# Prompt attention ordered by query halves of both heads, with two projection quarters behind each product with v

## What is computed

```python
def _fox_attention(q, k, v, c_q, c_k, past):
    ...
        s = jnp.einsum('bqhd,bkhd->bhqk', q_blk, k).astype(jnp.float32) * scale
        s = s + cq_blk.astype(jnp.float32).transpose(0, 2, 1)[..., None] - ckT
        s = jnp.where(k_pos[None, :] <= q_pos[:, None], s, NEG_INF)
        p = jax.nn.softmax(s, axis=-1)
        return jnp.einsum('bhqk,bkhd->bqhd', p.astype(v.dtype), v)
```

## Time and profile before

| | |
|---|---|
| median of 3 executions | 2783.07 us (2780.73 to 2791.97) |
| profiled execution, device time | 2785.51 us |
| its span | 2784.0 us |
| TensorE busy | 2279.1 us, 82% of the span |
| VectorE, ScalarE, GpSimd busy | 1317.5, 1122.8, 214.3 us |
| attention of the 8 pairs | from 185.5 to 1166.2 us of the span |
| mean granted clock of TensorE | 0.906 of full |

### The profile page before, as it was taken

The page is one execution under the profiler, slowest core; times in us unless marked ns, Lnnn a source line. Parts: engine busy times, 40 slices in busy tenths (PEclk is TensorE's granted clock), DMA queues, the critical chain, the costliest instruction groups (busy, mean ns, idle before and its releaser), DMA issues. The chain is left out here.

```text
span 2784.0 us, 36577 instructions
## 1 busy us (share of the span) xinstructions
PE 2279.1 (82%) x11080; PEld 1757.0 (63%) x11080; DVE 1317.5 (47%) x1548; ACT 1122.8 (40%) x1520; POOL 214.3 (8%) x278
## 2 busy tenths in 40 slices
PE   4468787888879797699899959989917999999991
PEld 2447575655657474499888849974515766666660
DVE  4333534444353435421156542111136888777874
ACT  3223333433334333221155642101106777777760
POOL 0210202011010101000012100000020000000002
PEclk9769898989889798799999979999958999999995
DMA  2210202021120201121145632123037999999986
GB/s 83 64 39 1 78 0 78 0 78 39 39 57 21 63 0 55 56 78 45 46 149 174 190 131 77 45 105 135 1 128 260 382 366 366 371 353 369 356 305 233
DMA packets 207115, 377.28 MB, mean 136 GB/s; under 512 B 20508, under 2 KB 128200, under 8 KB 206968
## 3 DMA queue, kind: packets, MB, share of 16 engines
q1 hardware_dynamic: 184680, 302.07, 32.3%
q0 software_dynamic: 18784, 61.92, 7.0%
q10 hardware_dynamic: 3584, 12.58, 1.1%
HBM read 301.87 MB, written 74.66 MB: 135 GB/s over the span
## 5 line engine op out<-in xcount | busy, mean ns | idle before, releaser
L2117 DVE TENSOR_TENSOR e_w_lo<-e_raw,e_w_hi 128x2048 fp32r<-128x2048 f32 x192 | 436.5, 2289 | 126.0 <-ACT e_w_hi L2044 113.8
L2044 ACT CAST e_w_hi<-e_raw 128x2048 fp32r<-128x2048 f32 x192 | 366.6, 1911 | 149.5 <-DMA e_raw<-w_down_e 67.5
L101 PE MATMUL proj_ps<-w_qkv_hi,xh 128*128 128x384 f32 x544 | 219.7, 404 | 33.5 <-PEq L286 19.2
L1133 PE MATMUL out_ps<-mT 128*128 128x512 f32 (+3 forms) x384 | 187.7, 575 | 10.8 <-ACT mT L1333 10.1
L103 PE MATMUL proj_ps<-w_qkv_hi,xl 128*128 128x384 f32 x544 | 186.6, 343 | 0.0
L102 PE MATMUL proj_ps<-w_qkv_lo,xh 128*128 128x384 f32 x544 | 186.1, 342 | 0.0
L1057 PE MATMUL max_ps<-qk_high 66*128 66x512 f32 (+1 forms) x192 | 89.9, 468 | 73.9 <-DVE neg_part L1471 67.4
L101 PEld LDWEIGHTS proj_ps<-w_qkv_hi,xh 128*128 128x128 f32 x544 | 106.4, 196 | 61.3 <-issue 58.3
L1656 PE MATMUL m_prod<-m_w_o,mT 128*128 128x512 f32 (+1 forms) x288 | 128.1, 604 | 12.2 <-DMA m_w_o<-w_o 12.2
L1471 DVE TENSOR_REDUCE neg_part<-max_ps 128x1 f32<-128x512 f32 (+3 forms) x128 | 75.7, 591 | 130.8 <-PE max_ps L1057 69.8
L1333 ACT ACTIVATE mT<-st_ps 128x512 f32<-128x512 f32 x192 | 93.5, 490 | 90.5 <-PE st_ps L1118 51.2
(11 more groups left out here) (402 smaller groups left out, 5364.7 us busy)
## 6 DMA issues: line engine op xcount, KB each, us to landing
e_raw<-w_gate_e SPq DMA_DIRECT2D x64, 1024.0 KB, 14.1
e_raw<-w_up_e SPq DMA_DIRECT2D x64, 1024.0 KB, 14.7
e_raw<-w_down_e SPq DMA_DIRECT2D x64, 1024.0 KB, 13.5
slot_x<-zrows POOLq DMA_DIRECT2D x48, 440.0 KB, 6.4
e_x<-slot_x SPq DMA_DIRECT2D x33, 384.0 KB, 12.1
w_raw<-w_in SPq DMA_DIRECT2D x24, 512.0 KB, 4.5
slot_y<-e_y ACTq DMA_DIRECT2D x32, 384.0 KB, 6.1
slot_y<-zrows POOLq DMA_DIRECT2D x24, 352.0 KB, 9.5
```

The lines of the kernel that those rows point to most:

```text
L101: nc.tensor.matmul(out, a_hi, b_hi, start=start, stop=False)
L1133: te.matmul(out_ps[u % 2][:, q0 - c * BANK:BANK], v_one[:, j, h, :], probsT[s % 2][:, 0:q1 - q0], start=(j == 0), stop=(s == last_step(u)) ...
L2044: sc.copy(w_hi[u][:, :], w.raw[c][:, :]).then_inc(wh_ready, 1)
L2117: v.tensor_tensor(w_lo[u][:, :], w.raw[c][:, :], w_hi[u][:, :], ALU.subtract).then_inc(wl_ready, 1)
```

## The change

Four things change in `attend`, and the work is the same.

- **Units.** They run (head 0, half 0), (head 1, half 0), (head 0, half 1), (head 1, half 1): 4, 4, 8 and 8 steps. The 24 maxima follow that order: 0 to 3 for the first unit, 4 to 7 for the second, 8 to 15 and 16 to 23.
- **Quarters.** All 36 stand right behind `weigh(s)` in steps 0 to 17, two in each. None stands in part 0 any more.
- **Items.** `SLOTS` is new. Before the loop, both heads are turned for the first four tiles only, and 4 maxima are taken instead of 10; in the loop `qk` 2 and 3 are the pair's own (steps 0 and 1 for head 0, 7 and 8 for head 1), `qk` 0 and 1 the next pair's. Eight maxima stand in steps 0 to 3 of the pair, four in steps 18 to 21.
- **GpSimd.** `take_v` copies four tiles at a time and waits for the steps that have used them; its first waits no longer for `kv_ready`, that is for the norms of the next pair.

```diff
-    UNITS = [(0, 0), (0, 1), (1, 0), (1, 1)]
+    UNITS = [(0, 0), (1, 0), (0, 1), (1, 1)]
...
-    PROJECT = {3: (1, 2), 4: (1, 2), 5: (1, 2), 6: (1, 1), 7: (1, 2), 8: (1, 1),
-               9: (1, 2), 10: (1, 1), 11: (1, 2), 12: (1, 2), 13: (1, 1), 14: (1, 2), 15: (1, 2), 16: (0, 1)}
+    PROJECT_STEPS = 18
...
-    SLOTS = {0: ((), (("qk1", 0), ("max", 10))), 1: ((("max", 11),), (("qk1", 1),)),
...
+    SLOTS = {0: ((), (("qk0", 2), ("max", 4))), 1: ((("max", 5),), (("qk0", 3), ("max", 6))),
...
-    FIRST_MAXES = 10
+    FIRST_MAXES = 4
...
-                def take_v(p, h):
-                    po.tensor_copy(v_one[:, :, h, rows_of(h)], v_next[:, 0:PT, rows_of(h)]).then_inc(v_copied[h], 1)
+                def take_v(p, h, half):
+                    tiles = slice(half * HALF, (half + 1) * HALF)
+                    po.tensor_copy(v_one[:, tiles, h, rows_of(h)], v_next[:, tiles, rows_of(h)]).then_inc(v_copied[h], 1)
...
-                    pool.wait_ge(st_ready, i * NS + last_step(1) + 1)
+                    pool.wait_ge(st_ready, i * NS + last_step(2) + 1)
                     alone(pool, g)
                     load_c(i + 1, 0)
+                    taken(HALF)
+                    weighed(last_step(2) - HALF)
+                    take_v(i + 1, 0, 0)
                     copy_high(i + 1, 0, 0)
-                    pool.wait_ge(kv_ready, i * BATCHES + 2 * BATCHES)
-                    alone(pool, g)
-                    pool.wait_ge(pv_done, i * NS + last_step(1) + 1)
-                    alone(pool, g)
-                    take_v(i + 1, 0)
+                    weighed(last_step(3) - HALF)
+                    take_v(i + 1, 1, 0)
                     if more:
                         rest_w(i + 2, 0)
                         rest_w(i + 2, 1)
+                    taken(NT)
+                    take_v(i + 1, 0, 1)
...
-                            if c == 0:
-                                pe.wait_ge(v_copied[h], i + 1)
-                                alone(pe, g)
+                        if j == c * HALF:
+                            pe.wait_ge(v_copied[h], i * 2 + c + 1)
+                            alone(pe, g)
...
-                        counts = PROJECT[s] if ahead and s in PROJECT else (0, 0)
+                        counts = (0, 2) if ahead and s < PROJECT_STEPS else (0, 0)
```

More of the change, by code:

```diff
@@ L808, in attend @@
-    FIRST_MAXES = 10
+    HALF = PT // 2
+    SLOTS = {0: ((), (("qk0", 2), ("max", 4))), 1: ((("max", 5),), (("qk0", 3), ("max", 6))),
+             2: ((("max", 7),), (("rows", 1), ("max", 8))), 3: ((("max", 9),), (("qs", 0), ("max", 10))),
+             4: ((("max", 11),), (("past", 0), ("max", 12))), 5: ((("max", 13),), (("past", 1), ("max", 14))),
+             6: ((("max", 15),), (("rows", 2), ("out", 0))), 7: ((("qk1", 2),), (("ss", 0), ("mean", 0))),
+             8: ((("qk1", 3),), (("sp", 0), ("max", 16))), 9: ((("max", 17), ("root", 0)), (("ss", 1),)),
+             10: ((("max", 18), ("sw", 0)), (("sp", 1),)), 11: ((("max", 19), ("past", 2)), (("sw", 1), ("norm", 0))),
+             12: ((("max", 20),), (("ss", 2), ("max", 21))),
+             13: ((("max", 22), ("sp", 2)), (("past", 3), ("max", 23), ("norm", 1))),
+             14: ((("rows", 3),), (("sw", 2), ("out", 1))), 15: ((), (("out", 2),)),
+             16: ((("qk0", 0),), (("ss", 3),)), 17: ((("qk0", 1),), (("sp", 3), ("mean", 1))),
+             18: ((("max", 0), ("w", 0)), (("sw", 3), ("ss", 4), ("root", 1))),
+             19: ((("max", 1), ("norm", 2)), (("sp", 4), ("w", 1))), 20: ((("max", 2), ("norm", 3)), (("sw", 4),)),
+             21: ((("max", 3),), (("w", 2),)), 22: ((("rows", 0),), (("qk1", 0), ("sum", 0))),
+             23: ((("qk1", 1),), (("o", 0),))}
@@ L809, in attend @@
+    FIRST_MAXES = 4
     NO_TURN = ("max", "out", "mean", "root", "norm", "w", "sum")
-    later = lambda item: item[0] in ("qk0", "mean", "root", "norm", "w") or item == ("rows", 0) or (item[0] == "max" and item[1] < FIRST_MAXES)
+    later = lambda item: item[0] in ("mean", "root", "norm", "w") or item == ("rows", 0) or \
+        (item[0] == "max" and item[1] < FIRST_MAXES) or (item[0] in ("qk0", "qk1") and item[1] < BATCHES // 2)
     items = lambda s, part, ahead: [e for e in SLOTS[s][part] if ahead or not later(e)]
@@ L1081, in _ @@
                     max_chunk(n)
[L1082 to L1084 removed]
+                pe.wait_ge(max_taken, FIRST_MAXES)
+                pe.wait_ge(turn_taken[0], in_bank(BATCHES, 0))
+                turn_rows(0, 0)
                 def step(i, ahead):
@@ L1525, in fill @@
                             h = int(what == "qk1")
-                            p, bank = i + 1 - h, use[item] % 2
+                            p, bank = i + 1 if n < BATCHES // 2 else i, use[item] % 2
                             take_cross(p, h, n, bank)
```

102 lines of the change are left out of this document (49 added, 53 removed), and 3 rows, old and new, of the table SLOTS.

## The result

The changed kernel takes 2837.05 us (median of three runs, 2830.97 to 2858.07) against 2783.07: a ratio of 1.0204, 95% interval 1.0115 to 1.0293. Slower, and 1 us above the range of the prediction. The first fence is the head of the page of its profile. The second is the timeline of TensorE (start, us, instruction, wait ahead of it): first the item `o` of the first and sixth pair, then rows of the third pair.

A forecast was written before the change was run, and what follows sets the result against it. TensorE was taken to wait for rounds through ScalarE and VectorE. Stretches 27.4 + 78.8 + 24.0 = 130.2 against 127.4, +2.8 a pair; 16.8 + 1.1 + 5 - 0.3 = +22.6, giving 2806 us, range 2764 to 2836.

The forecast's parts named there:

- Stretch A: From score(0) to score(4), the start of step 3; forecast to grow from 16.2 to 27.4 us.
- the walk with both falls of the clock: Walk through steps 0 to 2 with the clock falling after both max waits: score(4) at 28.7 us, 25.1 with none.
- the quarters stand ahead of the turn: Steps 0 to 2: quarters are not between turn and max, so hide none of the 2.3 us wait at max 5.
- Stretch B: From score(4) to score(19), the middle of a pair; forecast to fall from 87.2 to 78.8 us.
- the round from max to max is 1.45 us, against 0.8 of work: 0.65 each, five times, 3.3: New waits in the middle of a pair, with only a score between one step's last max and the next's early one.
- The terms for the bank: Middle of a pair: the wait for the projection's bank, 1.9 us, was to go.
- Stretch C: From score(19) to the next pair's score(0); forecast unchanged at 24.0 us, bounds 21.5 and 26.
- Without anything else in its way this comes to 21.5: End of a pair: the chain from max 3 through rows 0, turn, copy, subtraction, sum and `o` to score(0), 21.5 us.
- Last and seventh pair: Last pair, which projects nothing: +5 us, bounds 0 and +12; seventh, without weight blocks and its end shorter: +1.1.
- So this costs nothing: All steps: no quarter stands between score and product, but a weigh needs an exp one step older; put at nothing.
- Slower still: Rival, chance 0.1: clock stays low from `root` to step 3; C 26, A 30, +6 a pair, 2828 us.
- The cover works: Rival, chance 0.2: clock holds in A (25.1), norms precede weight blocks (C 21.5); -2.8 a pair, 2767 us.

The follow-up runs named there:

- e6: The changed kernel with both quarters moved from behind the product with v to ahead of it; 2773 us, 1.000 to the kernel before.
- e3: The changed kernel with VectorE's sum of squares behind the maxima of its step, except in steps 7 and 17; 2828 us, ratio 1.019 to the kernel before.
- e2: The changed kernel with GpSimd waiting for the next pair's norms ahead of its weight blocks, as before the change; 2860 us, ratio 1.025.
- e11: e8 with the last norm moved from step 20, ahead of max 3, to behind `o` at the pair's end; 2691 us, ratio 0.969 to the kernel before.
- e5: The changed kernel with the sum over the stream's chunks one step earlier, in step 21 instead of 22; 2851 us, ratio 1.028 to the kernel before.
- e4: The kernel before, with all quarters of a step behind weigh(s) and none ahead; 2823 us, ratio 1.018 to the kernel before.
- e8: e7 with the max ahead of the turn in steps 0 and 1; 2701 us, ratio 0.976 to the kernel before.
- e12: e11 with both quarters ahead of the product with v in steps 0 and 1; 2684 us, ratio 0.969 to the kernel before.
- e7: The changed kernel with one quarter either side of the product, plus the edits of e3 and e5; 2726 us, ratio 0.985 to the kernel before.

## Why the prediction was wrong

The direction was right: slower, by the mechanism given most weight, TensorE waiting for rounds through VectorE that no quarter covers. The size was not: +9.4 us a pair against +2.8. The attention as a whole grew by 74 us against 23; that the total grew by 54 only is the luck of 20 us in the experts behind it. By stretches, each mean against the mean of before, A grew by 10.9 us where 11.2 were forecast, B fell by 4.6 where 8.4 were, and C grew by 3.0 where 0 was: the miss is in B and C.

*Stretch A: right in its steps, and by some luck in its mean.* 27.4 forecast, 27.6 measured, with waits of 2.5 and 3.3 us at max 5 and 7 (2.3 and 3.6 forecast), and the clock at 0.65 right behind the second, after 1.00. But no pair has 27.6: three have 29, near the 28.7 of the walk with both falls of the clock, and three 26.2, where the clock came back 1.3 us sooner in the quarters behind weigh(0) and held behind max 5. Why it did so in these three was not found. The cited rule, that VectorE's copying out of PSUM between groups of matmuls does not cool the engine (the Trainium skill, TensorE: Matmul & The Clock Gate, loop structure), would have had A at 25.1; this trace speaks against it behind max 7, and behind max 5 in the third pair, for rounds that TensorE has to wait out; in the sixth pair the clock stayed at 1.00 behind the same 2.47 us. What A's walk took as given, that "the quarters stand ahead of the turn" and hide nothing, was the price of the change itself: e6, with the turn ahead of the quarters, has 18.3.

*Stretch B: 78.8 forecast, 83.5 measured.* The step that failed is "the round from max to max is 1.45 us, against 0.8 of work: 0.65 each, five times, 3.3". It counted TensorE and the maximum, not what stands ahead of it on VectorE: in every second step the sum of squares of the finished tile, itself behind ScalarE. The waits are 1.15 us in the mean, up to 1.7, and 5.8 a pair in place of 3.3. The wait for row 3 was 1.9 in place of 1.0, for the same reason. e3 took that queue away: 80.1, and a mean wait of 0.74. Of the other 1.3 us, 0.9 is that the sum started from the third pair, 87.2, where the mean is 88.1; for the rest no cause was separated. The terms for the bank (none left), row 2 (1.5 for 1.35) and `out 1` (1.5 at weigh(16)) held.

*Stretch C: 24.0 forecast, within 21.5 to 26; 27.0 measured.* "Without anything else in its way this comes to 21.5" was the error. The norms were stretched, 1.93 and 3.00 us, 3.3 more in all against the "up to 3.1" forecast, and so the rule on the shared port (the Trainium skill, SBUF — State Buffer, who interferes with whom) agrees with the trace. What the stall alone costs C stays open: e2 brought another delay with it, and e11 moved the whole norm. What the sum left out is the order behind max 3: `rows`, the turn, ScalarE's copies, the cross product, then the sum, then `o`, from 592.86 (max 3 on VectorE) to 602.96. There the sum waits behind a cross product that itself waits 5.1 us for ScalarE. e5 put the sum ahead and had 24.6, so at least 2.4 of the 3.0 us missed are this place in the queue.

*Last and seventh pair.* +5 forecast, +9.9 measured (93.8 us against 83.9; A +4.9, B +3.3, rest +1.7); the seventh +8.7 against +1.1: A +8.2, B -2.1, C +2.6. Ahead of the loop -0.7 against -0.3.

*"So this costs nothing": a term put at nothing.* That a product waits for an exp a step older holds in B, where no product waits for its exp. But the sentence stood for the whole order, and there was no term for a step whose two quarters stand together. e4 measured it in the old order: 8.1 us a pair, through three kinds of round. The prediction saw two of them in its own waits view, and priced only those it walked past.

*The rivals.* "Slower still" had 2828, for a clock that stays low from the root on. C went beyond its 26, but by the chain. That rival was also added up wrong: A 30 and C 26 are +7.4 a pair by the prediction's own terms, not +6, and give some 2838 us, beyond the 2836 at which the range ends. The measured 2837 lies there by coincidence, as A stayed under 30 and B went 4.7 over. The draw's +8 adds up to +5, which changes nothing. "The cover works" fell: the clock was not held behind max 7, A stayed above 25, and C did not come near 21.5.

## What to carry to other kernels

An independent piece of work on an in-order engine was worth most here between the two ends of a round through other engines. Before moving it, list every round (max to max, turn to max, exp to transpose, bank to bank) and what lies under it before and after; two pieces together cover one round, apart two. Then price a round from the queue of the engine that answers, the instructions ahead of the one waited for included: three reorderings were here worth 12.3 us a pair, the split of the quarters 13.9. And expect part of what one wait gives to come back at the next.

## What the hardware showed that was not expected

*The loop's turn on ScalarE.* Its first instruction of a pair in the loop is a table load of 1.28 us, in every kernel. At the start of the fourth pair of e8 it came 5.7 us after the last copy, 3.8 after score(0); in e12 3.2 us after the last copy, 0.9 after score(0). The profile shows nothing that it waited for in e8 ("issue"). Windows just ahead of it, e8 and then e12:

```profile
537.00:540.00 3.00, 1.26 (x3) 0.61 (x3) 1.87 (x7) 0.10 (x1) 0.95 (x2) 0.81 1.10 286
540.00:543.00 3.00, 3.00 (x11) 2.42 (x10) 3.00 (x1) 0.23 (x1) 0.00 (x0) 0.50 0.86 218
```

```profile
521.00:524.00 3.00, 1.25 (x6) 0.73 (x6) 1.87 (x7) 0.09 (x1) 0.79 (x2) 1.00 0.03 7
```

Late where the DMA engines are full (1.10 and 0.86), early where they are empty (0.03). In e11 (0.32 and 0.01 there) the load comes 1.4 us behind score(0), but 4.9 behind the last copy, so it tells less: a fixed time of some 5 us from the last copy would fit that run too, and only the 3.2 of e12 speaks against it. That busy DMA engines delay the loop's turn would fit all of these, and what e5 and e7 lost in A and e11 won; no run took the transfers away alone, so it stays open.

*A stretched sum.* Four small VectorE products took 1.25 us in the changed kernel and 4.16 in e5, beside GpSimd's DMA issues and weight block. The norms grew by 1.2 and 2.0 us in the same way. It is not the issues as such: the first three products of e5 took 0.29 us each beside them, as without them, and the fourth 3.20 us, from 597.32 to 600.52, when the weight block ended at 600.42. But this fourth product began 0.7 us before the block did, and what held it that long the trace does not say.
